# Sparse attention: queries split with tokens on partitions and turned by one transposing DMA a head

## The reference

```python
q, kc, vc, ks, vs, kw, vw, gl, z = jnp.split(h @ w_in, splits, axis=-1)
q  = rope(rms_norm(q.reshape(B, S, 16, 96), g_q), pos, 24)     # 16 heads, 4 groups of keys
ks = rope(rms_norm(ks.reshape(B, S, 4, 96), g_k[1]), pos, 24)  # selected branch
kw = rope(rms_norm(kw.reshape(B, S, 4, 96), g_k[2]), pos, 24)  # window branch
k_cmp, v_cmp = compress(kc, ...), compress(vc, ...)            # 31 compressed tokens
o_c = softmax(q . k_cmp) @ v_cmp
o_s = softmax(q . ks, causal) @ vs    # 512 tokens: all 8 blocks of keys are selected
o_w = softmax(q . kw, causal) @ vw    # and the window of 512 holds all of them
o = (g0 * o_c + g1 * o_s + g2 * o_w) * silu(z)
x = x + o @ w_out
```

## Time and profile before

| what | value |
|---|---|
| median of 3 runs | 877.67 us (877.56 to 878.72) |
| span of the profiled execution | 877.1 us |
| TensorE busy | 858.3 us (98%) |
| VectorE, ScalarE, GpSimd busy | 562.5, 501.1, 485.3 us |
| sixteen heads of attention | from about 680 to 826 us |
| granted TensorE clock, mean | 1.000 |

### The profile page before, as it was taken

The page is one execution under the profiler, slowest core; times in us unless marked ns, Lnnn a source line. Parts: engine busy times, 40 slices in busy tenths (PEclk is TensorE's granted clock), DMA queues, the critical chain, the costliest instruction groups (busy, mean ns, idle before and its releaser), DMA issues.

```text
span 877.1 us, 17413 instructions
## 1 busy us (share of the span) xinstructions
PE 858.3 (98%) x6361; PEld 719.9 (82%) x6361; DVE 562.5 (64%) x1607; ACT 501.1 (57%) x1151; POOL 485.3 (55%) x627
## 2 busy tenths in 40 slices
PE   6999999999999999999999999999999999999998
PEld 6999998888888888788888888778877677777786
DVE  4899988787888787562111113577698778788521
ACT  5456667877787878641233223344443888878610
POOL 2000407876867676454246443565684799888631
PEclk9999999999999999999999999999999999999999
DMA  6433322111110101123238212123321100100011
GB/s 214 130 97 97 97 78 90 36 40 53 40 52 13 53 14 49 49 96 96 94 98 170 93 57 86 55 89 103 96 94 51 50 3 2 51 3 2 3 49 48
DMA packets 39326, 58.97 MB, mean 67 GB/s; under 512 B 8757, under 2 KB 22346, under 8 KB 39242
## 3 DMA queue, kind: packets, MB, share of 16 engines
q1 hardware_dynamic: 39200, 57.85, 20.9%
q10 hardware_dynamic: 42, 0.01, 0.0%
HBM read 55.63 MB, written 2.10 MB: 66 GB/s over the span
## 4 chain that ended last, share of the span: by engine, by line
PE 85%; DVE 8%; ACT 3%; issue 2%; POOL 1%; DMA 0%; ACTq 0%; DVEq 0%; POOLq 0%
PE bank L97 19%; PE bank L99 18%; PE bank L98 18%; PE bank L1281 4%; PE bank L592 2%; PE bank L591 2%; DVE w_lo L2181 2%; PE bank L484 2%; PE bank L502 2%; PE bank L1264 2%; PE bank L511 2%; PE bank L503 2%; PE bank L1232 1%; PE bank L1233 1%; DVE w_raw L2197 1%
## 5 line engine op out<-in xcount | busy, mean ns | idle before, releaser
L2004 POOL TENSOR_TENSOR w_lo<-w_raw,w_hi 128x2048 fp32r<-128x2048 f32 (+1 forms) x26 | 118.4, 4553 | 123.9 <-ACT w_hi L1729 123.9
L97 PE MATMUL bank<-w_hi,h_hi 128*128 128x512 f32 (+3 forms) x472 | 171.4, 363 | 1.7 <-DVE h_lo L2101 1.0
L99 PE MATMUL bank<-w_hi,h_lo 128*128 128x512 f32 (+3 forms) x472 | 166.8, 353 | 0.0
L98 PE MATMUL bank<-w_lo,h_hi 128*128 128x512 f32 (+3 forms) x472 | 166.8, 353 | 0.0
L1729 ACT ACTIVATE w_hi<-w_raw 128x2048 fp32r<-128x2048 f32 (+1 forms) x26 | 49.2, 1892 | 94.0 <-PE bank L99 94.0
L97 PEld LDWEIGHTS bank<-w_hi,h_hi 128*128 128x128 f32 x472 | 88.7, 188 | 15.0 <-issue 3.4
L790 POOL TENSOR_TENSOR p<-kvr,p 128x512 f16<-128x512 f32 (+1 forms) x96 | 88.5, 943 | 18.4 <-ACT p L706 18.3
L99 PEld LDWEIGHTS bank<-w_hi,h_lo 128*128 128x128 f32 x472 | 88.7, 188 | 11.6
L98 PEld LDWEIGHTS bank<-w_lo,h_hi 128*128 128x128 f32 x472 | 88.9, 188 | 10.0
L97 PE MATMUL bank<-w_hi,o_hi 128*128 128x512 f32 x192 | 77.2, 402 | 0.8 <-DVE o_lo L2341 0.8
L99 PE MATMUL bank<-w_hi,o_lo 128*128 128x512 f32 x192 | 75.8, 395 | 0.0
(11 more groups left out here) (365 smaller groups left out, 2407.5 us busy)
## 6 DMA issues: line engine op xcount, KB each, us to landing
w_raw<-in_nsa_w_in SPq DMA_DIRECT2D x10, 1024.0 KB, 5.0
w_raw<-in_mla_w_in SPq DMA_DIRECT2D x8, 1024.0 KB, 5.1
w_raw<-in_mla_w_out SPq DMA_DIRECT2D x8, 1024.0 KB, 5.0
w_raw<-in_nsa_w_in SPq DMA_DIRECT2D x8, 984.0 KB, 5.0
w_raw<-in_nsa_w_out SPq DMA_DIRECT2D x4, 1024.0 KB, 5.6
w_raw<-in_mla_w_uq SPq DMA_DIRECT2D x7, 576.0 KB, 4.2
w_raw<-in_mla_w_ukv SPq DMA_DIRECT2D x15, 256.0 KB, 2.7
w_raw<-in_mla_w_in SPq DMA_DIRECT2D x4, 704.0 KB, 5.7
```

Source lines behind the costliest of these rows:

```text
L97: nc.tensor.matmul(out, a[0], b[0], start=start, stop=False)
L98: nc.tensor.matmul(out, a[0], b[1], start=False, stop=False)
L99: return nc.tensor.matmul(out, a[1], b[0], start=False, stop=stop)
L2004: nc.gpsimd.tensor_tensor(w_lo[g % 2][:, :, 0:width], w_raw[g % 2][:, :, 0:width], w_hi[g % 2][:, :, 0:width].bitcast(F32), ALU.subtract). ...
```

## The change

Queries are split in their own layout and turned afterwards. ScalarE's `high(n)` rounds the 4 x 96 columns of head n in `qs` to float16 into a staging buffer `q16` (128 partitions, high and low, 4 tiles, 128 columns, of which the last 32 are cleared once). VectorE's `q_low` writes the difference beside it. One transposing DMA on SP's queue turns all of it (128 x 1024 values of 2 bytes) into `qT`, high and low plane. Staging is double (`QS = 2`), `qT` threefold (`QR = 3`), and both work two heads ahead instead of one; heads 0 and 1 are prepared in the input projection. TensorE's `turn_q`, and with it its waits for `c_left` and for `q_lo`, is gone.

```diff
-                    qT_hi = [at_slab(f"qT_hi{a}", 20 + 4 * a, [DK + 2, SEQ], F16) for a in range(2)]
-                    qT_lo = [at_slab(f"qT_lo{a}", 22 + 4 * a, [DK, SEQ], F16) for a in range(2)]
+                    QR, QS = 3, 2
+                    qT = [at_slab(f"qT{a}", 114 + 2 * a, [P, 2, SEQ], F16) for a in range(QR)]
+                    qT_hi = lambda n: qT[n % QR][0:DK + 2, 0, :]
+                    qT_lo = lambda n: qT[n % QR][0:DK, 1, :]
+                    q16 = [at_slab(f"q16_{a}", 128 + 2 * a, [P, 2, NT, P], F16) for a in range(QS)]
+                    q_head = lambda n: qs[:, :, n * DK:(n + 1) * DK]
...
+                    def turn_q(sp, n):
+                        if n == 0:
+                            sp.wait_ge(rows_set, 2)
+                        sp.wait_ge(q_lo, n + 1)
+                        if n:
+                            sp.wait_ge(q_landed, 16 * n)
+                        if n >= QR:
+                            sp.wait_ge(s_done, U * (n - QR + 1))
+                        sp.dma_start_transpose(qT[n % QR][:, :, :].rearrange("d s (t c) -> d (s t) c", t=NT),
+                                               q16[n % QS][:, :, :, :].rearrange("p s t d -> p (s t d)")
+                                               ).then_inc(q_landed, 16)
                     def sync(sp):
+                        for n in range(QS, H):
+                            turn_q(sp, n)
...
                             if u == 0:
-                                pe.wait_ge(q_hi, n + 1)
+                                pe.wait_ge(q_landed, 16 * (n + 1))
...
                                 mask(n, u)
-                                if u == 0 and n + 1 < H:
-                                    turn_q(n + 1)
...
                             pe.wait_ge(c_exp, n + 1)
-                            pe.wait_ge(q_lo, min(n + 2, H))
...
                         def high(n):
-                            act.wait_ge(q_turned, n + 1)
-                            nc.scalar.activation(qT_hi[n % 2][0:DK, :], x_bank[0:DK, :], ACT.Copy).then_inc(q_hi, 1)
+                            if n % HPG == 0:
+                                act.wait_ge(normed1, KCMP + 1 + NT * (n // HPG + 1))
+                            if n >= QS:
+                                act.wait_ge(q_landed, 16 * (n - QS + 1))
+                            nc.scalar.activation(q16[n % QS][:, 0, :, 0:DK], q_head(n), ACT.Copy).then_inc(q_hi, 1)
...
                                 exponential(n, 0)
-                                if n + 1 < H:
-                                    high(n + 1)
+                                if n + QS < H:
+                                    high(n + QS)
...
+                    def q_low(dve, n):
+                        dve.wait_ge(q_hi, n + 1)
+                        at = q16[n % QS]
+                        nc.vector.tensor_tensor(at[:, 1, :, 0:DK], q_head(n), at[:, 0, :, 0:DK],
+                                                ALU.subtract).then_inc(q_lo, 1)
...
+                            if n + QS < H:
+                                q_low(dve, n + QS)
                             if more:
-                                low(n + 1)
                                 maximum(n + 1, 0)
...
+                    def clear_pads():
+                        for a in range(QS):
+                            last = nc.gpsimd.memset(q16[a][:, :, :, DK:P], 0.0)
+                        last.then_inc(rows_set, 1)
...
+                    for n in range(2):
+                        turn_q(sp, n)
                     for j, src in enumerate(first_pieces(nsa_w_out[0], 0, CW)):
                         sp.wait_ge(m_lo, NM - 1 + j)
                         sp.dma_start(w_raw[j][:, :, :], src).then_inc(w_landed[j], 16)
...
-                              (7, 0, 3): turn_most, (7, 1, 3): spread_most,
-                              (NIN - 1, 0, NT - 1): turn_first_q}
+                              (7, 0, 3): turn_most, (7, 1, 3): spread_most}
...
-                                 14: [lambda n=n: square1(n) for n in range(17, 21)],
+                                 14: [lambda n=n: square1(n) for n in range(17, 21)] + [lambda n=n: q_high(n) for n in range(2)],
...
                             if s == 2 * NIN - 1:
-                                first_high()
                                 act.wait_ge(w_landed[0], 16)
...
                     pool.wait_ge(kt_turned, 2 * G)
+                    clear_pads()
                     for b in range(2):
                         nc.gpsimd.memset(v16_all(b)[:, :, :, DV:DV1], 1.0).then_inc(rows_set, 1)
...
-                              9: [lambda: most(0), lambda: most(1)], 20: [most_of_all], 27: [scale_of_values]}
+                              9: [lambda: most(0), lambda: most(1)], 20: [most_of_all], 22: [lambda: q_low(dve, 0), lambda: q_low(dve, 1)], 27: [scale_of_values]}
```

More of the change, by code:

```diff
@@ L428, in sparse_attention @@
                     ct_at, cv_at = x_bank[:, 0:P], bank[6][:, 2 * P - NT:2 * P + NT * DV]
-                    q_turned, q_hi, q_lo, rows_set = sem("q_turned1"), sem("q_hi1"), sem("q_lo1"), sem("rows_set1")
+                    q_hi, q_lo, q_landed, rows_set = (sem(n) for n in ("q_hi1", "q_lo1", "q_landed1", "rows_set1"))
                     f_done, max_done, m_turned, m_in = sem("f_done1"), sem("max_done1"), sem("m_turned1"), sem("m_in1")
@@ L459, in tensor, with first_scores @@
                     def tensor(pe):
[L460 to L464, removed]
+                        def first_scores(n, u):
+                            k = U * n + u
+                            i, branches = tile_of[u]
+                            tok, keys = slice(i * P, (i + 1) * P), (i + 1) * P
+                            if n == 0 and u == 0:
                                 pe.wait_ge(kt_hi, 2 * G + 1)
                                 pe.wait_ge(kt_lo, 2 * G + 1)
[L467 to L478, removed]
                             if u == 0:
-                                pe.wait_ge(q_hi, n + 1)
+                                pe.wait_ge(q_landed, 16 * (n + 1))
                             if k >= 2:
@@ L510, in large_term @@
                             dst = score_bank[(U * n + u) % 3][:, w * left:(w + 1) * left]
-                            nc.tensor.matmul(dst, kT_hi[0:rows, b, g, keys], qT_hi[a][0:rows, j * P:], start=False, stop=False)
+                            nc.tensor.matmul(dst, kT_hi[0:rows, b, g, keys], qT_hi(n)[0:rows, j * P:], start=False, stop=False)
                         def mask(n, u):
@@ L553, in compressed_scores @@
                                 dst = x_bank[:, i * 2 * NC:(i + 1) * 2 * NC]
-                                nc.tensor.matmul(dst, qT_hi[a][0:DK, tok], kcT[:, :, n // HPG, :], start=True, stop=False)
-                                last = nc.tensor.matmul(dst[:, 0:NC], qT_lo[a][:, tok], kcT[:, 0, n // HPG, :],
+                                nc.tensor.matmul(dst, qT_hi(n)[0:DK, tok], kcT[:, :, n // HPG, :], start=True, stop=False)
+                                last = nc.tensor.matmul(dst[:, 0:NC], qT_lo(n)[:, tok], kcT[:, 0, n // HPG, :],
                                                         start=False, stop=True)
@@ L582, in values @@
                                 pe.wait_ge(v_step, V_REST)
-                                pe.wait_ge(rows_set, 3)
+                                pe.wait_ge(rows_set, 4)
                             for b in branches:
@@ L687, in attend @@
                             out_products()
-                        return (lambda: turn_q(0)), ahead, attend
+                        return ahead, attend
                     def scalar(act):
                         def high(n):
-                            act.wait_ge(q_turned, n + 1)
-                            nc.scalar.activation(qT_hi[n % 2][0:DK, :], x_bank[0:DK, :], ACT.Copy).then_inc(q_hi, 1)
+                            if n % HPG == 0:
[3 more added lines that the diff above has]
+                            nc.scalar.activation(q16[n % QS][:, 0, :, 0:DK], q_head(n), ACT.Copy).then_inc(q_hi, 1)
                         def exponential(n, u):
@@ L767, in attend @@
                                 w_high(g)
-                        return (lambda: high(0)), attend
+                        return high, attend
                     def gpsimd(pool):
@@ L918, in vector @@
                         nc.vector.tensor_copy(identr[:, :], ident[:, :])
-                        low(0)
                         for u in range(U):
@@ L1448, in turn_k_cmp @@
                         nc.tensor.transpose(bank[4][0:DK, 0:P], kcmp[:, :], ident[:, :]).then_inc(kt_turned, 1)
-                    turn_first_q, ahead, attend = sparse_tensor(pe)
+                    ahead, attend = sparse_tensor(pe)
                     def turn_most():
@@ L1894, in _ @@
                     slots(step, KV0 + 1)
-                    first_high, attend = sparse_scalar(act)
+                    q_high, attend = sparse_scalar(act)
```

23 lines of the change are left out of this document (9 added, 14 removed).

## The result

The kernel after takes 888.0 us (median of 4 runs, 887.3 to 888.62) against 878.13 (877.56 to 878.72) for the kernel before beside it: a ratio of 1.0112, with a 95% interval of 1.0098 to 1.0127. It is slower by 1.1%, 9.9 us in the medians. The profiled executions have spans of 886.0 and 877.1 us, so 8.9 us is what the trace has to account for. Most of the missing 1.0 lies in the profiled execution of the kernel before: its span of 877.1 is as long as the longest of that kernel's later runs, whose spans go from 875.5 to 877.1 with a median of 876.4.

A forecast was written before the change was run, and what follows sets the result against it. Bound in each head: TensorE's own work and ScalarE's two exponentials meeting at score unit 3. Span 877.1 + 7.7 (late start) + 0.5 (split) + 0 (transposes) = 885.3; median 0.6 above, 885.9; range 878 to 903.

The forecast's parts named there:

- a late load at the start: Output weights' first load queues on SP behind two transposing DMAs that await the pads; first scores of unit 5 7.7 us late.
- The transposes worth nothing: Sixteen groups of four transposes leave TensorE: 0 gained, 7.0 us at the other end; as a rival on the path, 879.0.
- the wait at unit 3: In each head, TensorE's weight load for score unit 3 awaits ScalarE's second exponential; removed 0.44 becomes a wait of 0.45.
- The split beside GpSimd: VectorE's low part, both inputs in SBUF, is held up by GpSimd's subtraction; 0.5 us for all heads, between 0 and 1.5.
- The DMA's length: Each transposing DMA of 256 KB on SP's queue takes 4.3 us, with ends of 2.0 and 9.0.
- the issuing of the second DMA: On SP's queue at the start, about 0.6 us between the first DMA's landing and the load's issue.
- The first issue: First transposing DMA, behind GpSimd's last weight subtraction and two pad memsets, is issued at 667.4.
- The upper row for the DMA: A 1,152 KB load in 3,072 rows of 384 bytes takes 9.0 us; taken as the DMA's upper end.
- The cover of 7.9 us: In a steady head, up to 7.9 us from DMA issue to landing costs nothing; beyond, a head lasts L + 1.1.
- The clock: Rival: after TensorE idles some 6 us before its last input tile, clock falls to 1.2 GHz; 889, chance 0.15.
- The rival that ends faster: Heads shorten while the output-weight load is not late, needing pads cleared early or start loss under 5 us; 873.2, chance 0.10.

The follow-up runs named there:

- experiment 1: The kernel after, with GpSimd clearing the pads before its last weight subtraction rather than behind it: 877.29 us, ratio 0.9993 to the kernel before.
- experiment 2: The kernel after, pads still cleared late, with the first load of the output weights ahead of the two first transposing DMAs on SP's queue: 878.29 us, ratio 1.0004.
- experiment 3: The kernel after, with four transposes a head put back on TensorE at their old place, nobody reading the result: 887.16 us.
- experiment 4: The kernel after, with eight unread transposes a head on TensorE at the old place: 892.07 us.
- experiment 9: The kernel before, with the four transposes of every head but the first issued twice: 884.23 us, ratio 1.007.
- experiment 7: The kernel after, with each transposing DMA of heads 2 to 15 done twice, the second after the first landed: 887.18 us.
- experiment 8: The kernel after, with each transposing DMA of heads 2 to 15 done three times, each behind the landing before: 912.13 us.
- experiment 6: The kernel of experiment 1, with the first scores of the next head's units 0 and 1 moved ahead of score unit 3: 874.1 us, ratio 0.9952.
- experiment 10: The kernel of experiment 6, with the 16 value products of the second tile also ahead of score unit 3: 872.85 us, ratio 0.9943.

## Why the prediction held, step by step

The forecast was 885.9 (885.3 in the terms of the span) and the profiled span is 886.0; the median is 888.0. The mechanism held: nothing from the heads, a late load at the start. That the sum came out so close is in part luck, since a wait that was 0.8 us too long, 0.5 us that never came and a clock that was left out offset each other.

**The transposes worth nothing:** shown. The period stayed at 8.98, the wait at unit 3 appeared at 0.35 where 0.45 was said (with 0.15 more ahead of the value products), and experiments 1 to 4 and 9 agree from both sides. The share of TensorE in busy time and chain, 98% and 85%, pointed the other way.

**The split beside GpSimd:** the blocking was there (1.06 us where one alone takes 0.5), its price wasn't. I had put 0.5 us for all heads; with an unchanged period and all 8.9 us found ahead of head 0 it is close to 0. VectorE's idle stretch of 1.01 took all of it.

**The DMA's length:** 4.3 us was the estimate, 3.2 the median from issue to landing, nearer to the plain store of equal size (2.0) than I had placed it. The 1.0 us of moving that the prediction gives beside its lower end is a third of the measured time (256 KB in 3.2 us is 82 GB/s from issue to landing). The other mis-sized term is the issuing of the second DMA: 0.6 was said, and with its gaps it took 671.83 - 670.47 = 1.36. The first issue, 667.4, came at 667.29, and the load took 5.33 rather than 5.6. Together that is 0.1 + 1.1 - 0.8 + 0.3 = 0.7 us less; with the work on ScalarE and VectorE as long as forecast (6.27 for 6.3), the first scores of unit 5 came 6.9 us late rather than 7.7. The upper row for the DMA was also misread: the load of 1,152 KB moves 128 KB in a microsecond, as much as the store of 256 KB, and the 1,024 KB loads move 183. That is not three times as slow per byte, and 9.0 us was the time of 4.5 times the bytes.

**The cover of 7.9 us:** experiments 7 and 8 enclose it. With three DMAs the head lasts 10.56 us on average, 1.3 more than their 9.3, where I had said 1.1; part of this may be the clock, which was 0.83 or 0.84 in three of the 10 us windows between 710 and 820. The total was 912 and not 917, since three took 9.3 and not 10: 14 x (10.56 - 8.98) = 22.1 us. The spans differ by 23.9, and the rest lies behind the first scores of head 15 at 840.50, where the granted clock is 0.83 for 10 us.

**The clock:** given 0.15 as a rival with up to 3.1 us, it happened and cost 2.0. It belonged in the sum: an idle stretch of 6 us was itself forecast. 7.7 + 0.5 was predicted; 6.9 + 0 + 2.0 came. The total was right because the clock stood in for what the DMA and the subtractions didn't take. What is left between 886.0 and the median of 888.0 is that a run lies some 1.8 us above its own span, in both kernels (887.84 for the profiled one here, 878.2 for a span of 876.4 in the kernel before). The 0.6 that I took was the distance from the median of the runs to the span of one long execution.

**The rival that ends faster** named its own condition, that the pads are cleared early. Experiment 1 did it, and the time was 877.3, no gain: its other half, heads that shorten, was false. It became true only with the order changed (experiments 6 and 10).

## What to carry over

Before an engine's work is taken away, look at what its next wait is for: an engine that is 98% busy can meet another engine's chain at one instruction with no slack, and then added work costs its full length while removed work returns nothing until the order is changed so that something fills the hole. Here that was so to within 0.05 us; it was read from one head and held in experiments 3, 4 and 9. An operation that is moved to a DMA queue takes its waits along: what stands behind it in that queue (here a load issued 14 us early, now behind two memsets) is the place to look for the loss. Where you forecast an idle stretch of TensorE as long as the 6 us here, put the slower clock behind it into the sum.

## What the runs showed of the hardware

- A transposing DMA of 128 x 1024 fp16 from SBUF to SBUF took 3.2 us from issue to landing (median of 16, 3.0 to 5.0; 3.1 in the experiments, those with 30 and 44 too), mostly 1.24 us of the queue to issue, and added 1056 packets of under 512 bytes (16896 for sixteen).
- An idle stretch of 5.96 us left TensorE at a granted clock of 0.50, and it was back at 1.00 some 5 us after work began again; products of 512 columns took 0.43 us rather than 0.23. With 26 products in the stretch the clock stayed at 1.00. A stretch need not be that long: in the kernel with three DMAs the granted clock was 0.83 from 710 to 720 and from 730 to 740, though no wait between two matmuls was longer than 1.9 us from 700 to 740.
- VectorE's subtraction with both inputs in SBUF took 1.06 us beside a GpSimd subtraction and 0.5 beside a GpSimd operation of 128 x 4; nothing hung on it here. The Trainium skill (SBUF — State Buffer, SBUF: two separate sides) has the two engines lock one pair of ports against each other for a whole instruction. The row of 1.06 us agrees: GpSimd's subtraction ends at 773.75, and 0.42 us are left. The row of 1.01 for two doesn't show such a lock, since they began 0.25 us into GpSimd's operation of 1.01 us.
